# One of four weight sums moved from VectorE to an accumulating transfer, in the second MLP product of a streaming encoder step

## The reference, cut to what matters

```python
h = _layer_norm(ALPHA * h + (mix @ w_out + b_out), ln1_g, ln1_b)
f = jnp.square(jax.nn.relu(h @ w_mlp1 + b_mlp1)) @ w_mlp2 + b_mlp2   # (T,1024)@(1024,4096), (T,4096)@(4096,1024)
h = _layer_norm(ALPHA * h + f, ln2_g, ln2_b)
```

## Time and profile before

| | |
|---|---|
| median of 3 runs | 833.44 us (833.3 to 835.96) |
| the profiled execution's own time | 835.31 us |
| its span, first to last instruction | 833.6 us |
| PE busy | 800.9 us, 96% |
| VectorE busy | 508.7 us, 61% |
| ACT busy | 391.3 us, 47% |
| GpSimd busy | 114.0 us, 14% |
| mean granted TensorE clock | 0.986 |

### The profile page before, as it was taken

How to read it: one execution, slowest core, us unless ns; L and a number is a source line. 1 busy time by engine, 2 the same in 40 slices (tenths; PEclk the granted TensorE clock), 3 DMA queues, 4 the chain that set the end, 5 groups by cost and what they waited for, 6 DMA issues and landing times.

```text
span 833.6 us, 14313 instructions
## 1 busy us (share of the span) xinstructions
PE 800.9 (96%) x5787; PEld 770.2 (92%) x5787; DVE 508.7 (61%) x851; ACT 391.3 (47%) x653; POOL 114.0 (14%) x134
## 2 busy tenths in 40 slices
PE   4899999999999999999999999999999999999994
PEld 2789889999988899999998999999999999999994
DVE  6753424546454456875867689775667887455444
ACT  4542415555455465563544664333555433345333
POOL 5320000190000000006540000000000000000452
PEclk9799999999999999999999999999999999999997
DMA  9513232112111202234111214222221422222202
GB/s 352 197 35 135 69 113 69 44 39 80 52 51 51 75 28 76 77 110 144 51 52 34 88 57 152 77 102 71 83 69 57 152 77 102 76 75 81 72 28 87
DMA packets 23082, 71.62 MB, mean 86 GB/s; under 512 B 2464, under 2 KB 6704, under 8 KB 22640
## 3 DMA queue, kind: packets, MB, share of 16 engines
q1 hardware_dynamic: 22192, 67.97, 24.4%
q0 software_dynamic: 544, 2.52, 0.9%
q10 hardware_dynamic: 288, 0.33, 0.1%
HBM read 65.96 MB, written 4.85 MB: 85 GB/s over the span
## 4 chain that ended last, share of the span: by engine, by line
PE 94%; DVE 4%; ACT 1%; DMA 0%; issue 0%; POOL 0%; ACTq 0%
PE lin L582 14%; PE lin L583 14%; PE lin L584 14%; PE z L1015 5%; PE z L1017 5%; PE z L1018 5%; PE lin L920 3%; PE lin L921 3%; PE lin L922 3%; PE z L797 3%; PE lin L1061 2%; PE lin L1060 2%; PE lin L1059 2%; PE z L783 1%; PE z L852 1%; PE z L584 1%
## 5 line engine op out<-in xcount | busy, mean ns | idle before, releaser
L582 PE MATMUL lin<-h_hi,whi 128*128 128x288 f32 (+1 forms) x832 | 247.3, 297 | 0.0
L583 PE MATMUL lin<-h_lo,whi 128*128 128x288 f32 (+1 forms) x832 | 245.9, 296 | 0.0
L584 PE MATMUL lin<-h_hi,wlo 128*128 128x288 f32 (+1 forms) x832 | 245.0, 294 | 0.0
L582 PEld LDWEIGHTS lin<-h_hi,whi 128*128 128x128 f32 x832 | 156.5, 188 | 0.1
L584 PEld LDWEIGHTS lin<-h_hi,wlo 128*128 128x128 f32 x832 | 156.6, 188 | 0.0
L583 PEld LDWEIGHTS lin<-h_lo,whi 128*128 128x128 f32 x832 | 156.4, 188 | 0.1
L1696 DVE TENSOR_TENSOR wlo<-raw,whi 128x1024 fp32r<-128x1024 f32 x65 | 80.0, 1231 | 38.9 <-ACT whi L1092 33.8
L1092 ACT ACTIVATE whi<-raw 128x1024 fp32r<-128x1024 f32 x60 | 63.1, 1051 | 55.7 <-PE lin L584 32.6
L1505 ACT ACTIVATE relu_t<-lin,vecs 128x288 f32<-128x288 f32 x60 | 30.0, 501 | 89.8 <-PE lin L584 87.8
L1015 PE MATMUL z<-f_ops,whi 128*128 128x288 f32 x216 | 64.2, 297 | 1.4 <-issue 1.4
L2123 DVE TENSOR_TENSOR relu_sq<-relu_t 128x288 f32<-128x288 f32 x60 | 27.4, 457 | 59.7 <-ACT relu_t L1505 59.7
(11 more groups left out here) (332 smaller groups left out, 1922.2 us busy)
## 6 DMA issues: line engine op xcount, KB each, us to landing
raw<-w_stream SPq DMA_DIRECT2D x88, 512.0 KB, 3.5
w_set<-w_sets SPq DMA_DIRECT2D x32, 384.0 KB, 3.6
r<-x_t SPq DMA_DIRECT2D x8, 296.0 KB, 5.3
y<-r SPq DMA_DIRECT2D x16, 144.0 KB, 1.9
kcache<-k_cache SPq DMA_DIRECT2D x1, 2048.0 KB, 13.7
vcache<-v_cache SPq DMA_DIRECT2D x1, 2048.0 KB, 10.7
k_new<-k_t POOLq DMA_DIRECT2D x1, 1184.0 KB, 4.8
v_new<-v_t POOLq DMA_DIRECT2D x1, 1024.0 KB, 5.7
```

What stands on the lines that cost most here:

```text
L582: pe.matmul(out, w_h, hi, start=first, stop=False)
L583: pe.matmul(out, w_h, lo, start=False, stop=False)
L584: return pe.matmul(out, w_l, hi, start=False, stop=last)
```

## The change

Sum 1 is no longer an instruction of VectorE. Block BE is loaded straight into slot SI, and GpSimd then issues a second transfer that reads GA from DRAM and adds it to SI on the way in (`accum_op=ALU.add`). Slot BE is first written by sum 2. GpSimd's eight transfers (two passes of four groups) stand in its order after the first layer norm's work, each behind a wait for BE's landing, with new semaphores `s1_in`.

With it, waits and orders change. VectorE's sum 2 waits for `s1_in`, and so does ACT's `op_hi` of q = 3. For group 0, SI lies over `raw` slot 3, which holds the pass's last unit; so BE's load now waits for the split of that unit (`end - 1`), and comes last of the four, behind GA. For groups from 2 on BE's load waits for `op_lo` of q = 3 of group g-2 instead of sum 4. GA is read from DRAM twice.

```diff
             def load_set(s, g, i):
-                sp.dma_start(w_set[g % 2][:, i, :], w2_d[s, g, i]).then_inc(set_in[g % 2][i], 16)
+                at = SI if i == BE else i
+                sp.dma_start(w_set[g % 2][:, at, :], w2_d[s, g, i]).then_inc(set_in[g % 2][i], 16)
...
-                for i, u in ((AL, end - 4), (DE, end - 3), (BE, end - 2), (GA, end - 2)):
+                for i, u in ((AL, end - 4), (DE, end - 3), (GA, end - 2), (BE, end - 1)):
                     sp.wait_ge(lo_split, u + 1)
                     load_set(s, 0, i)
...
                     o = OPS * (GROUPS * s + g - 2)
-                    sp.wait_ge(s_made, 4 * (GROUPS * s + g - 2) + 4)
+
+                    sp.wait_ge(s_lo, o + 4)
                     load_set(s, g, BE)
...
+                elif q == 3:
+                    act.wait_ge(s1_in[g % 2], 16 * (n // 2 + 1))
                 else:
-                    act.wait_ge(s_made, 4 * n + (2, 1, 3, 4)[q - 2])
+                    act.wait_ge(s_made, 3 * n + (1, None, 2, 3)[q - 2])
...
-                if n == 1:
-                    dve.wait_ge(set_in[g % 2][BE], 16 * (done // 2 + 1))
-                    dve.wait_ge(set_in[g % 2][GA], 16 * (done // 2 + 1))
-                    out, a, b, op = SI, BE, GA, ALU.add
-                elif n == 2:
+                if n == 2:
+                    dve.wait_ge(s1_in[g % 2], 16 * (done // 2 + 1))
                     dve.wait_ge(set_in[g % 2][AL], 16 * (done // 2 + 1))
                     out, a, b, op = BE, SI, AL, ALU.add
                 elif n == 3:
+                    dve.wait_ge(set_in[g % 2][GA], 16 * (done // 2 + 1))
                     out, a, b, op = AL, BE, GA, ALU.subtract
...
-                        weight_sum(s, 0, 1)
+                        dve.wait_ge(lo_split, U_MLP1[s] + PASS_UNITS[s])
                         weight_sum(s, 0, 2)
...
-                    elif q == 6 and g + 1 < GROUPS:
-                        weight_sum(s, g + 1, 1)
...
+            for s in range(2):
+                for g in range(GROUPS):
+                    n = 16 * ((GROUPS * s + g) // 2 + 1)
+                    pool.wait_ge(set_in[g % 2][BE], n)
+                    pool.dma_start(w_set[g % 2][:, SI, :], w2_d[s, g, GA], accum_op=ALU.add).then_inc(s1_in[g % 2], 16)
```

More of the change, by code:

```diff
@@ L313, in encoder_step @@
         set_in = [[sem(f"set_in{e}_{i}") for i in range(4)] for e in range(2)]
+        s1_in = [sem("s1_in0"), sem("s1_in1")]
         s_made, s_hi, s_lo, op_done, r_added = (
@@ L2250, in weight_sum @@
                     out, a, b, op = DE, DE, BE, ALU.add
-                if n > 1:
-                    dve.wait_ge(s_made, 4 * done + min(n - 1, 2))
+                if n > 2:
+                    dve.wait_ge(s_made, 3 * done + 1)
                 tt(w[:, out, :], w[:, a, :], w[:, b, :], op).then_inc(s_made, 1)
```

## The result

The changed kernel took 836.79 us (median of 12 runs, 834.99 to 839.15), the kernel before 833.37 us (12 runs too): ratio 1.0038, interval 1.0027 to 1.0049. It is 3.4 us slower, 2.3 to 4.1 by the interval. 836.3 was forecast, in 833.0 to 840.8. The profiled execution took 836.61 us, its span is 834.9.

The account below looks back on a forecast made before the run. PE bounds the kernel, and VectorE matters only at operation 2 of each pass. Delays of 1.7 and 1.2 us there sum to +2.9 us, put on 833.44: median 836.3 us, range 833.0 to 840.8.

Parts of the forecast that it names:

- The serial chain: Last unit's split to group 0's sum 2: split, BE's load, wake-ups, adding transfer; sum 2 shifts by A - 3.60 us.
- A: Time of GpSimd's adding transfer from issue to landing, in no row; taken as 5.3 us, between two and three streams.
- the two-stream reading: Both source reads of the adding transfer share the engine's stream, two times 1.2 us, giving 4.7 us to landing.
- the 4.7 that was in the text: Adding transfer's us to landing by the skill's half-rate rule, giving a sum of +1.7 us.
- the second rival: Half-rate add, almost hidden: adding transfer lands in 4.2 to 5.0 us, cost +0.7 to +2.3 us; chance 0.28.
- 2A - 7.7: Total us added over both passes' group 0 shifts, less a 0.52 us hole in the second; +2.9 forecast.
- the prediction's own signs: Wrong if adding transfer under 4.6 or over 7.2 us, PE waits at another operation, or clock falls behind longer hole.
- the last rival: A long adding transfer, from 7.2 us on; at 9, +14 us, and PE's stall could lower the clock; chance 0.16.
- What the relief can bring: VectorE freed of sum 1 in group 0: at most 0.77 us in the first pass, nothing in the second.
- Group 1's cover: Slack before group 1's sum 2 delays operation 8: 1.9 us a pass, gone when the adding transfer takes over 7.2.
- The edits priced at nothing: Later groups' loads, SP's queue, GpSimd's issues, 3.1 MB more DRAM reads, VectorE's `lo_split` wait: no cost expected.

Follow-up runs that it names:

- Run 7: Changed kernel with group 0's adding transfer cut in two halves, the second issued when the first has landed; 846.12 against 834.42 us for before, ratio 1.0143.
- Run 5: Kernel before, with `add_op(0)` moved two low parts earlier in each pass; 834.26 against 834.42 us, ratio 0.9998.
- (1): Changed kernel with group 0's sum 1 back on VectorE, groups 1 to 3 keeping the transfer; 833.85 against 834.28 us for before, ratio 0.999.
- (2): Changed kernel with the adding transfer in group 0 only; 837.81 us, ratio 1.0037 against the kernel before.
- (3): Changed kernel with slots SI and BE exchanging roles, so the add is in place, a unit earlier; 833.21 against 834.28 us for before, ratio 0.9988.
- (4): Changed kernel with the add taken out: GpSimd copies GA over SI plainly, sum 1 lacking BE; 834.11 us, ratio 0.9992 against the kernel before.
- run 9: The changed kernel once more, unedited; 838.20 against 834.15 us for the kernel before, ratio 1.0049.
- run 8: Changed kernel with group 1's adding transfer cut in two serial halves; 842.04 us, ratio 1.0088 against the kernel before.
- 6: Kernel with SI and BE exchanging roles, but no GpSimd transfers and sum 1 left out; 833.64 against 834.42 us for before, ratio 0.9988.

## Why the prediction was right, point by point

- **What bounds it.** The only place where VectorE reaches PE is operation 2 of each pass, and every microsecond of delay there went into PE's wait: shifts of 1.24 and 1.73 - 0.52 us gave waits 1.25 and 1.13 us longer. Run 7 has nearly the same slope, 5.1 us into 4.9. Run 5 corrects the picture: behind `add_op(0)` stands `add_op(2)`, at nearly the same tightness. For the prediction, which moved all of it together, that made no difference.
- **The serial chain.** This was the cause, shown by three runs: without it in group 0 the loss is gone (1), with it there alone the loss is whole (2), and with the chain begun a unit earlier the same eight transfers leave PE waiting 0.7 us less than before (3).
- **A, the price of the adding transfer.** 5.3 was taken; 4.6 and 5.0 were measured. The plain transfer was put at 3.5 and is 3.2 (4); the second stream was put at 1.2 and costs 1.4 to 1.8. So the two-stream reading was the nearer one. The Trainium skill, "Collectives: The Full Stack", section "The bandwidth ceiling", says of the reduce step of a collective that an add needs two source reads through one ring. Run 4's difference agrees with it in size, 1.4 to 1.8 us where one stream was put at 1.2; that a second read is the cause, no run shows. I should have gone with the 4.7 that was in the text. By A the outcome fell into the bracket of the second rival (4.2 to 5.0, "almost hidden"), whose sum at 4.8 is +1.9 us.
- **The sum.** 2A - 7.7 with the measured landings is 1.9; the waits rose by 2.4, as the wake-ups took some tenths more; the time rose by 3.4. So the forecast of +2.9 was near with two errors of opposite sign: A too long by 0.5 (1.0 us), and the clock's fall behind a hole of 2.3 us left out. That they nearly cancel is luck. By the prediction's own signs it stood at the edge of being wrong: A under 4.6 was one, and 4.6 was measured in the first pass; the clock falling behind the longer hole was another, and run 9 shows it.
- **The clock.** I had put its fall only in the last rival, behind holes of 6 us and more, because the trace showed 1.00 behind 1.08 us and 0.50 behind 8.9 (of the 8 us at 0.50 in the earlier trace rows, 3.4 lie inside that hole, which ends at 23.39). But the trace of before had it behind 1.93 us too, at L920 (0.83 from 446 to 456), a row that I had set aside as "before all of this". Run 9 shows it behind 2.29, run 8 behind 1.76. A fall costs 1.5 us and is not always there, so that it makes up the missing microsecond fits its size, and run 9 leaves no steady loss beside it in the stretch that matters; the share of executions in which it happens is not known.
- **What the relief can bring.** At most 0.77 us was worked out; runs 3 and 6 show 0.7 us less waiting, and times 1.0 us lower, intervals 0.3 to 1.8; run 1, without less waiting, is 0.8 lower.
- **Group 1's cover** was mis-sized: 1.9 us in the text, 0.8 and 1.0 by run 8. GpSimd's issue, behind BE's landing, came at 513.25 and not 512.3, 0.7 us of it because operation 2 and all around it stand that much later in the profile of after, and the adding transfer took 8.4 us beside five others, where 7.3 was taken. Sum 2 waited 2.13 us, a little more than the 2 us given as a sign, and PE did not wait.
- **The edits priced at nothing** were nothing that the intervals of runs 1, 3 and 6 could tell.

## What to carry to other kernels

When work moves from a busy engine to a transfer, price the chain, not the work: from the event that lets the first transfer start to the instruction that needs the last one. Here 8.1 to 8.6 us of chain replaced one instruction of 0.95 us, and whether that costs depends on when the chain can begin; a slot that comes free one unit earlier turned 2.4 us more waiting into 0.7 us less. Before a stall on a sequence of instructions is attacked by reordering, look at what stands right behind the first waiter: the second one may be as tight. And price a hole in PE's work by its length and by what the clock may do behind it.

## What the runs showed of the hardware that was not expected

- An adding transfer of 384 KB from DRAM to SBUF, issued by GpSimd, landed 4.4 to 5.1 us after its issue when alone and, in group 1, 7.7 to 8.6 us beside other loads; without the add it was 3.2 us alone and 6.5 in group 1 (run 4). GpSimd was held for 0.85 to 0.94 us by its issue, and for 0.55 to 0.57 us by that of the plain one.
- The granted clock fell to the lower level behind holes of PE as short as 1.76 us (run 8) and 1.93 us (at L920), in some executions and not in others: behind 1.93 us in five of twelve profiles, and behind the 2.3 to 2.4 us before operation 2 of the first pass in one of four (run 9, and not after, 2 and 8). A fall cost 1.3 to 1.5 us behind these holes, and 1.6 and 2.5 us behind the 5.0 and 3.7 us of run 7. Behind holes of 1.49 us and less in this part of the kernel, the changed kernel's second pass among them, no profile has one.
